# Weaving layer one's prompt memory attention into the retention heads, with retention in six steps and two output tiles beside the last head

## The reference, cut to what matters

```python
z = rmsnorm(h, w['a_norm1'][a]) @ w['a_w_in'][a]          # q|k|v|gate of 6 heads x 128, and 256 memory queries
q = rope(z[..., :RET_W]...); k = rope(z[..., RET_W:2 * RET_W]...) * (RET_HD ** -0.5)
v = z[..., 2 * RET_W:3 * RET_W]; g = z[..., 3 * RET_W:4 * RET_W]; qm = z[..., 4 * RET_W:]
s_new, o = retention(ret_s0[a], q, k, v)                  # chunks of 128: masked q k^T v, plus q times the running state
mix = head_groupnorm(o).reshape(b, t, RET_W) * jax.nn.silu(g)
om = mem_attend(qm, mem_k[l], mem_v[l])                   # softmax over 256 memory rows, 4 heads x 64
h = h + jnp.concatenate([mix, om], axis=-1) @ w_out       # 1024 columns, 8 tiles of 128
u = rmsnorm(h, w['mlp_norm'][l]) @ w['w_up'][l]
h = h + jnp.square(jax.nn.relu(u)) @ w['w_down'][l]
```

## Time and profile before

| | |
|---|---|
| median of 3 runs | 1654.03 us (1651.86 to 1656.52) |
| the profiled execution: its time | 1651.49 us |
| its span, first to last instruction | 1649.7 us |
| TensorE busy | 1547.9 us, 94% |
| VectorE busy | 827.9 us, 50% |
| ScalarE busy | 565.6 us, 34% |
| mean granted TensorE clock | 0.97 of 2.4 GHz |
| last matmul of the last head's gate tile issued | 297.6 us from the span's start |
| first matmul of output tile 2 | 373.80 us |

### The profile page before, as it was taken

The page is one execution under the profiler, slowest core; times in us unless marked ns, Lnnn a source line. Parts: engine busy times, 40 slices in busy tenths (PEclk is TensorE's granted clock), DMA queues, the critical chain, the costliest instruction groups (busy, mean ns, idle before and its releaser), DMA issues.

```text
span 1649.7 us, 28864 instructions
## 1 busy us (share of the span) xinstructions
PE 1547.9 (94%) x11443; PEld 1438.9 (87%) x11443; DVE 827.9 (50%) x1288; ACT 565.6 (34%) x876; POOL 50.4 (3%) x76
## 2 busy tenths in 40 slices
PE   3899999779999999999999789999899999999998
PEld 3889999569999999999988457766799999999998
DVE  4846777635533433334576645655454334343344
ACT  4532222323422313223443135555243223132234
POOL 1120000010000000000001000000000000000000
PEclk8999999889999999999999889999999999999999
DMA  6543333122232332222324303543122223323221
GB/s 193 167 141 92 92 92 92 56 82 77 77 90 77 90 88 78 82 83 77 90 80 120 107 11 93 145 121 99 46 83 70 84 81 89 87 76 89 76 89 58
DMA packets 229383, 149.34 MB, mean 91 GB/s; under 512 B 11121, under 2 KB 222466, under 8 KB 229282
## 3 DMA queue, kind: packets, MB, share of 16 engines
q1 hardware_dynamic: 218802, 122.57, 25.8%
q0 software_dynamic: 6032, 20.28, 4.1%
q10 hardware_dynamic: 4448, 5.11, 0.9%
HBM read 140.26 MB, written 7.68 MB: 90 GB/s over the span
## 4 chain that ended last, share of the span: by engine, by line
PE 72%; DVE 5%; ACT 2%; issue 1%; ACTq 0%; DVEq 0%
PE ps L572 57%; PE ps L1064 3%; PE ps L1022 2%; PE ps L1091 2%; PE ps L1005 1%; PE ps L932 1%; PE ps L967 1%; PE ps L968 1%; DVE t L1858 1%; DVE wl L1566 1%; DVE rstd L1585 1%; PE ps L935 1%; PE ps L962 1%; PE ps L1000 0%; ACT wh L1172 0%
## 5 line engine op out<-in xcount | busy, mean ns | idle before, releaser
L572 PE MATMUL ps<-xh,wh 128*128 128x288 f32 x1542 | 334.5, 299 | 15.1 <-DVE wl L1566 15.1
L572 PE MATMUL ps<-mh,wh 128*128 128x288 f32 (+1 forms) x1424 | 325.3, 297 | 17.0 <-DVE wl L1566 13.7
L572 PE MATMUL ps<-xh,wl 128*128 128x288 f32 x1542 | 329.7, 295 | 0.0
L572 PE MATMUL ps<-xl,wh 128*128 128x288 f32 x1542 | 329.5, 295 | 0.0
L572 PE MATMUL ps<-ml,wh 128*128 128x288 f32 (+1 forms) x1424 | 322.9, 296 | 0.0
L572 PE MATMUL ps<-mh,wl 128*128 128x288 f32 (+1 forms) x1424 | 322.8, 295 | 0.0
L1172 ACT ACTIVATE wh<-raw 128x1024 fp32r<-128x1024 f32 (+1 forms) x195 | 202.1, 1036 | 286.0 <-PE ps L572 268.3
L1566 DVE TENSOR_TENSOR wl<-raw,wh 128x1024 fp32r<-128x1024 f32 (+1 forms) x195 | 233.0, 1195 | 74.0 <-ACT wh L1172 72.7
L572 PEld LDWEIGHTS ps<-xh,wh 128*128 128x128 f32 x1542 | 248.3, 190 | 20.6 <-DVE wl L1566 17.3
L572 PEld LDWEIGHTS ps<-mh,wh 128*128 128x128 f32 x1424 | 237.5, 190 | 19.9 <-DVE wl L1566 14.5
L572 PEld LDWEIGHTS ps<-xl,wh 128*128 128x128 f32 x1542 | 248.6, 189 | 0.0
(11 more groups left out here) (290 smaller groups left out, 1341.7 us busy)
## 6 DMA issues: line engine op xcount, KB each, us to landing
raw<-in_w_up SPq DMA_DIRECT2D x64, 512.0 KB, 4.0
raw<-in_w_down SPq DMA_DIRECT2D x64, 512.0 KB, 3.6
pages<-in_cache_mla SPq DMA_DIRECT2D x128, 160.0 KB, 2.2
raw<-in_a_w_in SPq DMA_DIRECT2D x26, 512.0 KB, 3.8
memkc<-in_cache_mem_k POOLq DMA_DIRECT2D x16, 256.0 KB, 4.6
memvc<-in_cache_mem_v POOLq DMA_DIRECT2D x16, 256.0 KB, 5.7
raw<-in_a_w_out SPq DMA_DIRECT2D x8, 512.0 KB, 3.7
raw<-in_b_w_out SPq DMA_DIRECT2D x8, 512.0 KB, 3.7
```

What stands on the lines that cost most here:

```text
L572: last = mm(ps[:, 2 * (m % 2) + c, 0:n], w[:, s, kk, :], x(kk, col, n), start=(kk == 0 and nth == 0), stop=(kk == k - 1 and nth == 2))
```

## The change

Three things change in layer one. The eight memory units move from behind the last head into the tiles of h=1 to h=5: unit u takes two neighbouring tiles of the sequence, from part 2 of h=1 on, so u=0 lies on parts 2 and 3 of h=1, u=1 on parts 0 and 1 of h=2, u=2 on parts 2 and 3 of h=2, and so on to u=7 on parts 0 and 1 of h=5. All of a unit is in bank 7, with one buffer `memE0` and one `memPT0` laid over `ss` and `sq`. Scores are issued in the middle of the even tile and the turn in the middle of the odd one; values come after the odd tile. VectorE takes the maximum in the middle of the even tile and normalises at its end, after that tile's retention step.

The retention step becomes six: `ret_rows` (in the middle of tile 0), `ret_scores` (after tile 0), `ret_kv` (in the middle of tile 1), `ret_update` (after tile 1), `ret_out` (after tile 2), `ret_back` (after tile 3), in banks 4 to 6. In VectorE's order a retention step of a tile now comes after that tile's eviction. The mix is written to `onorm` instead of `t1`.

Behind the last tile the six steps of the last head stand between parts of output tiles 0 and 1: all `kk` but 5 (that head's own) are issued as soon as the head before is there, and `kk` 5 of both at the end.

```diff
+def unit_of(h, part):
+    t = 4 * (h - 1) + part - 2
+    return t // 2 if 0 <= t < 2 * MEM_UNITS else None
...
 # TensorE
+            def unit_turn_a(u):
+                pe.wait_ge(me_norm, u + 1)
+                for r in range(2):
+                    for b in range(2):
+                        last = pe.transpose(ps[:, 7, P * (2 * r + b):P * (2 * r + b) + P], mem[0]["E"][:, b, P * r:P * r + P], ident[:, :])
+                last.then_inc(me_tr, 1)
...
             for h in range(1, H_RET):
+                for part in range(4):
+                    u = unit_of(h, part)
+                    def middle(h):
+                        if h == 0 and part == 0:
+                            sample_back(0, 1)
+                        if part < 2:
+                            (ret_rows, ret_kv)[part](h)
+                        if u is not None:
+                            (unit_scores_a, unit_turn_a)[part % 2](u)
                     z_tile(h, part, middle)
-                    if (h, part) == (H_RET - 1, 3):
-                        mem_step(0, 0)
-                        mem_step(0, 1)
-                    if end:
-                        end(h - 1)
-            last_head = {2: ret_rows, 4: ret_kv, 6: ret_out, 9: ret_back}
-            for k in range(2, 12):
-                mem_step(0, k)
-                if k in last_head:
-                    last_head[k](H_RET - 1)
+                    (ret_scores, ret_update, ret_out, ret_back)[part](h - 1)
+                    if u is not None and part % 2:
+                        unit_values_a(u)
+            last = H_RET - 1
+            ret_rows(last)
+            pe.wait_ge(me_lo, MEM_UNITS)
+            pe.wait_ge(r_lo, last)
+            out_part(0, 0, 1, 2)
+            ret_scores(last)
+            out_part(0, 3, 4)
+            ret_kv(last)
+            out_part(0, 6, 7)
+            ret_update(last)
+            out_part(1, 0, 1, 2)
+            ret_out(last)
+            out_part(1, 3, 4, 6, 7)
+            ret_back(last)
+            pe.wait_ge(r_lo, H_RET)
+            for j in range(2):
+                out_part(j, last)
...
 # ScalarE: middle of tile 0 ret_rows, middle of the even tile exp, of the odd tile the copy; then
+                    if part >= 2:
+                        (ret_out, ret_back)[part - 2](h - 1)
+                    if u is not None and part % 2:
+                        unit_values_a(u)
+            w_head(M_OUT[0] + 1)
+            ret_rows(last)
+            ret_out(last)
+            ret_back(last)
...
 # VectorE, z_tile: w_tail(m + 1); middle; the eviction; then
+                if end:
+                    end(h - 1)
+                if part == 3:
                     dve.wait_ge(gate_tanh, h + 1)
                     do(stt(dst, t2[:, :], 1.0, t1[:, :], ALU.add, ALU.mult))
...
+                    def middle(h):
+                        if h == 0 and part == 0:
+                            sample_low(0, 1)
+                        if part < 2:
+                            (ret_rows, ret_kv)[part](h)
+                        if u is not None and part % 2 == 0:
+                            unit_max_a(u)
+                    def end(h):
+                        (ret_scores, ret_update, ret_out, ret_back)[part](h)
+                        if u is not None:
+                            (unit_norm_a, unit_values_a)[part % 2](u)
+                    z_tile(h, part, middle, end)
+            w_tail(M_OUT[0] + 1)
+            for step in (ret_rows, ret_scores, ret_kv, ret_update, ret_out, ret_back):
+                step(last)
```

More of the change, by code:

```diff
@@ L319, in build @@
         s_out = sem("s_out")
-        r_rows, r_act, r_dve, r_kv, r_state, r_o = (
-            sem(f"r_{n}") for n in ("rows", "act", "dve", "kv", "state", "o"))
+        r_rows, r_act, r_dve, r_sc, r_masked, r_kv, r_st, r_up, r_state, r_o = (
+            sem(f"r_{n}") for n in ("rows", "act", "dve", "sc", "masked", "kv", "st", "up", "state", "o"))
         r_var, r_std, r_norm, r_back, r_mix, r_hi, r_lo = (
@@ L554, in _, with dense @@
             mm = pe.matmul
-            def dense(m, hi, lo, n=HALF, i=None, ready=None, k=None, part=None, half=None):
+            def dense(m, hi, lo, n=HALF, i=None, ready=None, k=None, part=None, half=None, final=None):
                 k = k or k_tiles(m)
                 part = part or range(k)
+                final = k - 1 if final is None else final
                 if 0 in part and half != 1:
@@ L672, in sample_keys, with unit_values_a @@
+            def unit_values_a(u):
+                a = u % 2
+                pe.wait_ge(me_pt, u + 1)
+                for b in range(2):
+                    h = a + 2 * b
+                    for r in range(2):
+                        last = mm(ps[64 * a:64 * a + 64, 7, P * b:P * b + P], mrow[:, 0, r, MEM_W + 64 * h:MEM_W + 64 * h + 64],
+                                  mem[0]["PT"][:, r, P * b:P * b + P], start=(r == 0), stop=(r == 1))
+                last.then_inc(me_pv, 1)
             def sample_keys(layer, b):
@@ L757, in ret_kv, with ret_update @@
                         rows = slice(32 * half, 32 * half + 32)
-                        last = mm(ps[rows, 7, 0:P], qexp[:, 4 * half + b, :], s0[:, 4 * half + b, :], start=False, stop=(b == NB // 2 - 1))
+                        last = mm(ps[rows, 6, 0:P], qexp[:, 4 * half + b, :], s0[:, 4 * half + b, :], start=False, stop=(b == NB // 2 - 1))
                 last.then_inc(r_kv, 1)
+            def ret_update(h):
+                pe.wait_ge(r_masked, h + 1)
+                pe.wait_ge(r_st, h + 1)
+                for half in range(2):
+                    rows = slice(32 * half, 32 * half + 32)
+                    last = mm(ps[:, 4 + half, :], krs[rows, :], vexp[rows, :, :].rearrange("p b e -> p (b e)"), start=True, stop=True)
+                last.then_inc(r_up, 1)
             def ret_out(h):
@@ new lines, in out_part @@
+            def out_part(j, *part):
+                dense(M_OUT[0] + j, tiles(mh), tiles(ml), part=part, final=H_RET - 1)
+            last = H_RET - 1
[10 more added lines that the diff above has]
+            ret_out(last)
@@ L1215, in _, with unit_exp_a, unit_turn_a, unit_values_a @@
                     do(f(mrow[:, m // 4, :, col:col + P], ps[:, 6 + m % 2, 0:2 * P].rearrange("p (r d) -> p r d", r=2), ACT.Copy), C[kv_rows])
[L1217 to L1237, removed]
+            def unit_exp_a(u):
+                act.wait_ge(me_max, u + 1)
+                for b in range(2):
+                    do(f(mem[0]["E"][:, b, :], ps[:, 7, 256 * b:256 * b + 256], ACT.Exp,
+                         bias=vec[:, 4 + b:5 + b], scale=MEM_SCALE, accum_out=vec[:, 8 + b:9 + b]), C[me_exp] if b else own)
+            def unit_turn_a(u):
+                act.wait_ge(me_tr, u + 1)
+                do(f(mem[0]["PT"][:, :, :], ps[:, 7, :].rearrange("p (r c) -> p r c", r=2), ACT.Copy), C[me_pt])
+            def unit_values_a(u):
+                i, rows = u // 2, slice(64 * (u % 2), 64 * (u % 2) + 64)
+                act.wait_ge(me_pv, u + 1)
+                do(f(mh[rows, 6:8, P * i:P * i + P], ps[rows, 7, 0:2 * P].rearrange("p (b r) -> p b r", b=2), ACT.Copy), C[me_hi])
             def sample_keys(layer, b):
@@ L1312, in _ @@
             for h in range(1, H_RET):
-                for part, (middle, end) in enumerate(((first_back if h == 1 else None, ret_rows), (None, ret_kv), (ret_out, None), (ret_back, None))):
-                    z_tile(h, part, middle)
[L1315 to L1319, removed]
-            last_head = {2: ret_rows, 4: ret_kv, 6: ret_out, 9: ret_back}
-            for k in range(2, 12):
-                mem_step(0, k)
-                if k == 4:
-                    w_head(M_OUT[0] + 1)
-                if k in last_head:
-                    last_head[k](H_RET - 1)
+                for part in range(4):
+                    u = unit_of(h, part)
+                    def middle(h):
+                        if h == 0 and part == 0:
+                            sample_heads(0, 1)
+                        if part == 0:
+                            ret_rows(h)
+                        if u is not None:
+                            (unit_exp_a, unit_turn_a)[part % 2](u)
+                    z_tile(h, part, middle)
+                    if part >= 2:
+                        (ret_out, ret_back)[part - 2](h - 1)
+                    if u is not None and part % 2:
+                        unit_values_a(u)
+            last = H_RET - 1
+            w_head(M_OUT[0] + 1)
+            ret_rows(last)
+            ret_out(last)
+            ret_back(last)
             def out_and_mlp(layer, g_next):
@@ L1707, in ret_kv, with ret_update @@
                     dve.wait_ge(s_out, 32 * h)
[L1708 removed]
+                do(copy(st[:, 0, :], ps[:, 5, 0:P]))
                 for n in range(1, RT):
[L1710 removed]
```

(31 more changed lines are left out.)

144 lines of the change are left out of this document (48 added, 96 removed).

## The result

The changed kernel takes 1659.24 us (median of 18, 1655.36 to 1660.95) against 1653.88 us for the kernel before, measured beside it. The ratio is 1.0034 (95% interval 1.0026 to 1.0043): slower by 5.4 us. The profiled execution took 1656.26 us.

A forecast was written before the change was run, and what follows sets the result against it. TensorE was taken to set the end throughout. Tail -76.2 + 36.0, units +21.3, head 5 -1.5, waits +16.5, half clock +8.4 and +0.8 gave +5.3 us: 1659.3 on the median, range 1647 to 1668 (8 in 10).

The forecast's parts named there:

- Units +21.3: Heads: eight memory units at 2.66 us each lengthen the heads by 21.3 us, as TensorE has no room.
- waits +16.5: Heads: TensorE waits at the turn of units 0, 2, 4, 6 for VectorE's late product; net 4 x 4.1 us.
- half clock +8.4: Heads: matmuls after each of the four new waits run at half clock, 2.1 us each, 8.4 in all.
- less 1.5: Head 5: `ret_back` of head 4 and its delay are counted in the tail instead, -1.5 us.
- thin margin: Heads, parts 0 and 1: product ready at 16.0 us, turn reached at 17.4, a margin of 1.4 us.
- rival 3: Heads: margin gone on parts 0 and 1, more waits and longer half clock; 1668 us; 0.18 shared with another rival.
- Rival 2: Heads: even units' product ready when TensorE reaches the turn; saves 16.5 + 8.4 us more, 1634 us; chance 0.10.
- the clock digits between 140 and 290 us: Heads: profile sign of half clock after the long waits; the slices' digits fall from 9 to 8.
- 36.0 us: Tail: output tile 2 starts 36.0 us after the last issue of the last gate tile, instead of 76.2.
- The evicted gate tile is there at 1.0: Tail: the last gate tile is evicted 1.0 us after its last issue.
- the first three `kk`: Tail, output tile 0: `kk` 0 to 2 take 2.4 us, from 4.5 to 7.0.
- The waits of 4.0: Tail: TensorE waits 4.0 us for the last head's head norm, whose rows come at 25.8.

The follow-up runs named there:

- experiment 1: Changed kernel with VectorE normalising the unit ahead of the retention step on part 2, not behind the head norm: 1633.2 us, 0.9872 of the kernel before.
- experiment 5: Changed kernel with VectorE's split of output tile 0's weights moved behind head 4's mix: 1655.15 us, 1.0008 of the kernel before.
- experiment 2: Changed kernel with 32 needless matmuls before the turn of units 0, 2, 4, 6: 1650.9 us, 0.9983 of the kernel before.
- the last version: Changed kernel with normalisation before the head norm, output tile 0's split behind head 4's mix, and a reordered tail: 1623.2 us, 0.9809 of the kernel before.

## Why the prediction was right, point by point

I forecast 1659.3 us and slower as the likeliest case. The median is 1659.24, nearer than the terms deserve; the part of that which is luck is told under "The rest". The terms:

- **Heads.** Units +21.3, waits +16.5, half clock +8.4, less 1.5: I had +44.7. From the first tile of h=1 (123.81, now 123.41) to the last issue of the last gate tile (297.6, now 342.03) the traces have +44.8. The bracket of 4.70 us, four times, is the one I gave. The units on parts 0 and 1 show none: their product is ready 1.0 us before the turn (320.73 and 321.74 for unit 7), where I had 1.4. So the thin margin held and rival 3 is out. That rival's 5 us for the clock did not follow from its own "up to 4 us of cost after each", which is 7.6 more than my sum had.
- **Rival 2** (the product is ready in time) was right in its price: experiment 1 gained 26 us where I had 24.9. It was wrong in its condition, as VectorE's written order said.
- **A sign that failed.** I wanted the clock digits between 140 and 290 us to fall from 9 to 8. They stayed at 9 (the fourth to the seventh): a slice is 41 us long and the stretch at half clock some 7 us at most, which leaves over 0.9. The pairs in the timeline are the sign that counts.

```profile
PEclk8999999998999999999999889999999999999999
```

- **Tail.** I had 36.0 us and it is 39.4. The step that failed is "The evicted gate tile is there at 1.0": it was there at 2.7. In the trace of the kernel before VectorE was free at that moment, and the eviction was done at 298.72, 1.1 us behind the last gate tile. Here the head norm of head 4 had kept it till 342.71, and then, in its written order, the split of output tile 0's weights stands ahead of the eviction:

```profile
342.75 1.23 DVE L1582 TENSOR_TENSOR wl<-raw,wh 128x1024 fp32r<-128x1024 f32 x1
344.01 0.76 DVE L1606 TENSOR_TENSOR t<-ps,rstd 128x576 f32<-128x576 f32 x1
344.80 0.76 DVE L1764 SCALAR_TENSOR_TENSOR onorm<-ps,z 128x576 f32<-128x576 f32 x1
347.64 0.76 DVE L1766 TENSOR_TENSOR ml<-onorm,mh 128x576 fp32r<-128x576 f32 x1 [2.08 <-ACT mh L1291]
```

  On the eviction hangs ScalarE's tanh with its table load, on that the high part of head 4 and then the low part. It ends at 348.40, 6.4 us behind the last gate tile, where I had 4.5, and output tile 0 starts 0.10 us later. It is this chain that sets the start, not `ret_rows`: in experiment 5 `ret_rows` ran at full clock and was done a microsecond before the low part, and TensorE waited. I also priced the first three `kk` at full clock; they went at half:

```profile
345.70 1.09 PE L729 MATMUL ps<-ident,z 128*128 128x128 f32 x4 [2.08 <-DVE onorm L1764]
...
348.50 0.82 PE L579 MATMUL ps<-mh,wh 128*128 128x288 f32 x2
349.12 0.68 PE L579 MATMUL ps<-ml,wh 128*128 128x288 f32 x2
```

  The late low part is 1.9 us, the half clock 1.5 (3.9 us from 348.50 to 352.43, where I had 2.4). So `ret_scores` starts at 10.4 instead of 7.0, and the 3.4 us stay to the end. The waits of 4.0 (3.77 by bracket), 2.5 (2.56) and 4 (3.46) are close to what I had.
- **The rest.** Up to output tile 2 I had +4.5 and the pair of traces has +7.6. From there to the end nothing is changed, and yet the changed kernel's execution took 1273.1 us and that of before 1275.9. The clock is what differs. This is one wait of 1.30 us, in the same place of both programs, first in the kernel before and then in the changed one:

```profile
1179.20 0.57 PE L572 MATMUL ps<-mh,wh 128*128 128x288 f32 x1 [1.30 <-DVE ml L2093]
1179.57 0.44 PE L572 MATMUL ps<-ml,wh 128*128 128x288 f32 x1
```

```profile
1185.26 0.40 PE L579 MATMUL ps<-mh,wh 128*128 128x288 f32 x1 [1.30 <-DVE ml L2124]
1185.49 0.29 PE L579 MATMUL ps<-ml,wh 128*128 128x288 f32 x1
```

  Behind it the one went at half clock until 1182.7, the other at full, and the next wait was over 9.9 us later in the one and 8.4 in the other: 1.5 us from this place alone. Over the eight profiled kernels of this case that rest takes from 1273.1 to 1277.2, so two single executions cannot settle 3 us; the medians, over 18 runs each, say +5.4. In the pair of traces the tail's error of 3.4 us was thus mostly offset by a clock that stayed up more often behind it, which I had not forecast: that is luck. Whether the medians owe their agreement to the same thing is not shown; the profiled execution of the changed kernel (granted clock 0.971) was 3 us faster than its median, and most of its 18 have 0.968 or 0.969.
- **The rule of the Trainium skill** ("TensorE: Matmul & The Clock Gate", "HAM oscillation — how this bites in real kernels"), that recurring waits send the engine back to half rate each time, held in all four heads (0.48 us a pair behind each wait of 4.70); experiment 2 prices it at 8.3 us.

## What to carry to other kernels

When work is woven into a full engine, look at the helper engine's written order at each place where the full engine will wait: two operations of 0.9 us behind a 6.8 us chain made this change a loss of 5 us, and the same two ahead of it make it a gain of 21. Price a wait on TensorE with the matmuls that follow it, too: here each wait of 4.7 us cost 1.4 to 2.7 more. And walk the helper engine's queue instruction by instruction at the seams, with all that hangs on each result. The split that I passed over stands in the same place in every tile. At the last one it held up the eviction, and with it tanh, the low part of head 4 and the first output tile.

## What I had not expected of the hardware

I had looked for half clock only behind waits of 2.5 us and more. In the last version it came behind two short ones: TensorE had been idle for 0.58 and 1.01 us (before 317.34 and 319.21), and from the first row below on the steps are long, until 326.9. `ret_scores`, eight matmuls that take 1.05 us at full clock, took 1.91 us.

```profile
319.67 0.78 PE L731 MATMUL ps<-ident,z 128*128 128x128 f32 x4
...
320.80 0.48 PE L734 MATMUL ps<-z 128*64 128x64 f32 x2
321.81 0.82 PE L579 MATMUL ps<-mh,wh 128*128 128x288 f32 x2 [0.53 <-issue]
...
324.82 1.91 PE L740 MATMUL ps<-z 128*128 128x128 f32 x8
```

The same two idles left `ret_rows` at full clock in experiment 5, where the fall came behind a third, of 1.06 us; and the wait of 1.30 us shown under "The rest" was followed by half clock in one execution and by full clock in another. So the length of a wait does not say by itself what follows it.

And the fall can come late: in the last version the matmuls behind a wait of 4.13 us (349.52) began 0.26 us apart, at full clock, and fell to 0.48 only 1.2 us on.
